# High and low halves of the weights interleaved column by column, with a shifted base and new homes for the early raw units

## What is computed

```python
mod = silu_c @ w_mod[l] + b_mod[l]
...
z_rec = h @ w_in[:, :REC_COLS]
z_rest = h @ w_in[:, REC_COLS:]
merged = jax.nn.sigmoid(ga) * (y_a @ w_pa) + jax.nn.sigmoid(gb) * (y_b @ w_pb)
return merged @ w_o, s_f, s_b
...
a, b = jnp.split(h @ w_up, 2, axis=-1)
return (jax.nn.silu(a) * b) @ w_down
...
proj = jnp.einsum('btd,de->bte', u, w_in[l])
y = jnp.einsum('bte,ed->btd', mixed, w_out[l])
```

## Time and profile before

| | us |
|---|---|
| median of 2 runs | 2324.36 |
| the runs | 2323.56 and 2325.15 |
| span of the profiled execution | 2323.0 |
| TensorE matmuls busy | 2264.8 |
| VectorE busy | 1633.6 |
| ScalarE busy | 995.5 |

### The profile page before, as it was taken

How to read it: one execution, slowest core, us unless ns; L and a number is a source line. 1 busy time by engine, 2 the same in 40 slices (tenths; PEclk the granted TensorE clock), 3 DMA queues, 4 the chain that set the end, 5 groups by cost and what they waited for, 6 DMA issues and landing times.

```text
span 2323.0 us, 48644 instructions
## 1 busy us (share of the span) xinstructions
PE 2264.8 (97%) x18378; PEld 2180.9 (94%) x18378; DVE 1633.6 (70%) x2515; ACT 995.5 (43%) x1402; POOL 8.4 (0%) x18
## 2 busy tenths in 40 slices
PE   5899999999999999989999999999999999999999
PEld 3678888999999999989999999999999999999999
DVE  4465564899976666988888887865557666667764
ACT  3322222555543434454444444444445444444452
POOL 0000000000000000000000000000000000000000
PEclk8999999999999999999999999999999999999999
DMA  9965455444356667975454555555556444444443
GB/s 406 389 252 218 181 223 210 164 145 144 144 217 236 258 236 287 344 306 197 181 181 181 185 187 188 185 198 180 184 192 217 156 153 147 160 146 161 146 179 128
DMA packets 69511, 475.62 MB, mean 205 GB/s; under 512 B 7728, under 2 KB 9776, under 8 KB 18384
## 3 DMA queue, kind: packets, MB, share of 16 engines
q1 hardware_dynamic: 68688, 467.59, 54.9%
q0 software_dynamic: 768, 7.26, 0.9%
HBM read 469.58 MB, written 5.24 MB: 204 GB/s over the span
## 4 chain that ended last, share of the span: by engine, by line
PE 88%; DVE 4%; ACT 1%; issue 1%; DVEq 0%; ACTq 0%
PE acc L795 83%; PE aux L795 4%; DVE lo L1157 1%; DVE ar L1384 0%; DVE qla L1377 0%; PE aux L1052 0%; ACT hi L462 0%; DVE raw L1167 0%; DVE qlb L1377 0%; DVE qs L1426 0%; DVE hxu L1174 0%; ACT n L666 0%; DVE n L1498 0%; ACT tt L594 0%; PE aux L887 0%
## 5 line engine op out<-in xcount | busy, mean ns | idle before, releaser
L1157 DVE TENSOR_TENSOR lo<-raw,hi 128x1024 fp32r<-128x1024 f32 (+1 forms) x716 | 811.9, 1167 | 196.8 <-ACT hi L462 192.2
L462 ACT ACTIVATE hi<-raw 128x1024 fp32r<-128x1024 f32 (+1 forms) x716 | 695.7, 1012 | 313.9 <-PE acc L795 259.9
L795 PE MATMUL acc<-hx,hi 128*128 128x256 f32 (+1 forms) x3072 | 662.7, 312 | 7.5 <-DVE lo L1157 4.1
L795 PEld LDWEIGHTS acc<-hx,hi 128*128 128x128 f32 x3072 | 496.1, 189 | 44.4 <-issue 6.9
L795 PE MATMUL acc<-hxu,hi 128*128 128x256 f32 x2816 | 502.7, 282 | 7.6 <-DVE hxu L1174 7.5
L795 PE MATMUL acc<-hx,lo 128*128 128x256 f32 (+1 forms) x1536 | 474.2, 309 | 0.0
L795 PEld LDWEIGHTS acc<-hxu,hi 128*128 128x128 f32 x2816 | 432.5, 189 | 8.8 <-issue 7.4
L795 PE MATMUL acc<-hxu,lo 128*128 128x256 f32 x1408 | 394.5, 280 | 0.0
L795 PE MATMUL acc<-u,hi 128*128 128x272 f32 (+1 forms) x2048 | 382.3, 287 | 0.0
L795 PEld LDWEIGHTS acc<-u,hi 128*128 128x128 f32 x2048 | 317.4, 188 | 4.5 <-issue 2.5
L795 PEld LDWEIGHTS acc<-hx,lo 128*128 128x128 f32 x1536 | 289.5, 189 | 17.5
(11 more groups left out here) (291 smaller groups left out, 2285.0 us busy)
## 6 DMA issues: line engine op xcount, KB each, us to landing
raw<-wts SPq DMA_DIRECT2D x390, 1024.0 KB, 4.8
raw<-wdown SPq DMA_DIRECT2D x64, 704.0 KB, 4.1
xc<-xct SPq DMA_DIRECT2D x1, 4096.0 KB, 12.3
rawx<-wts SPq DMA_DIRECT2D x2, 1024.0 KB, 24.7
x<-xct SPq DMA_DIRECT2D x1, 2048.0 KB, 9.8
park<-x POOLq DMA_DIRECT2D x1, 2048.0 KB, 10.4
xf<-park POOLq DMA_DIRECT2D x1, 2048.0 KB, 9.6
outt<-outs SPq DMA_DIRECT2D x16, 128.0 KB, 3.3
```

Of the source, the lines that this page charges most:

```text
L462: A.activation(HI[:, slot, a:b, 0:P], RAW[:, p % 4, a:b, :], ACT.Copy).then_inc(hi_half, 1)
L795: return pe.matmul(*a, **k)
L1157: V.tensor_tensor(LO[:, slot, a:b, 0:P], RAW[:, p % 4, a:b, :], HI[:, slot, a:b, 0:P].bitcast(F32), ALU.subtract).then_inc(lo_half, 1)
```

## The change

HI and LO become one tile HL in which column c of the high half and column c of the low half are neighbours: a row for one k has 2 x 128 + 16 = 272 words (1088 bytes). `half` is the view that ScalarE and VectorE write and read, `weights` the 128 columns, two words apart, that a matmul loads. HL starts at 32 KiB + 64 bytes and ends where HX begins. RAWX becomes two places of 8 KiB at 193 and 168, away from the weights. The second lies over SQ1, so SP waits for `sq1_read` to reach 4 before it loads it; the wait between the two early `lo` halves goes.

```diff
-PW = P + 8
+PAIR = 2 * P + 16
+HLROW = 2 * 16 * PAIR - 16
...
-        HI = at("hi", 32, [P, 2, 16, PW], F32R)
-        LO = at("lo", 49, [P, 2, 16, PW], F32R)
+        HL = at("hl", 32 + 1 / 16, [P, HLROW], F32R)
...
-        RAWX = at("rawx", 49.5, [P, 2, 17, P])
+        RAWX = [at("rawx0", 193, [P, 16, P]), at("rawx1", 168, [P, 16, P])]
...
+        def half(slot, a, b, part):
+
+            first = (slot * 16 + a) * PAIR + part
+            return bass.AP(HL[:].tensor, first, [[HLROW, P], [PAIR, b - a], [2, P]])
+
+        def weights(slot, k, part):
+
+            first = (slot * 16 + k) * PAIR + part
+            return bass.AP(HL[:].tensor, first, [[HLROW, P], [2, P]])
...
             for s in range(2):
-                sp.dma_start(RAWX[:, s, 0:16, :], wts[UNIT0["rec"] + 2 * s]).then_inc(raw_early[s], 16)
+                if s:
+                    sp.wait_ge(sq1_read, 4)
+                sp.dma_start(RAWX[s][:], wts[UNIT0["rec"] + 2 * s]).then_inc(raw_early[s], 16)
...
-                    A.activation(HI[:, slot, a:b, 0:P], RAW[:, p % 4, a:b, :], ACT.Copy).then_inc(hi_half, 1)
+                    A.activation(half(slot, a, b, 0), RAW[:, p % 4, a:b, :], ACT.Copy).then_inc(hi_half, 1)
...
-                        mm(o, HI[:, slot, k, 0:P], xh(k), start=first, stop=False)
-                        mm(o, HI[:, slot, k, 0:P], xl(k), start=False, stop=False)
-                        ins = mm(o, LO[:, slot, k, 0:P], xh(k), start=False, stop=last)
+                        mm(o, weights(slot, k, 0), xh(k), start=first, stop=False)
+                        mm(o, weights(slot, k, 0), xl(k), start=False, stop=False)
+                        ins = mm(o, weights(slot, k, 1), xh(k), start=False, stop=last)
...
-                    V.tensor_tensor(LO[:, slot, a:b, 0:P], RAW[:, p % 4, a:b, :], HI[:, slot, a:b, 0:P].bitcast(F32),
+                    V.tensor_tensor(half(slot, a, b, 1), RAW[:, p % 4, a:b, :], half(slot, a, b, 0).bitcast(F32),
                                     ALU.subtract).then_inc(lo_half, 1)
...
                         dve.wait_ge(hi_half, 2 * (i - 1) + h + 1)
-                        if h:
-                            dve.wait_ge(lo_half, 2 * i - 1)
-                        V.tensor_tensor(LO[:, i - 1, a:b, 0:P], RAWX[:, i - 1, a:b, :], HI[:, i - 1, a:b, 0:P].bitcast(F32),
+                        V.tensor_tensor(half(i - 1, a, b, 1), RAWX[i - 1][:, a:b, :], half(i - 1, a, b, 0).bitcast(F32),
                                         ALU.subtract).then_inc(lo_half, 1)
```

More of the change, by code:

```diff
@@ L517, in _ @@
                     for a, b in ((0, 8), (8, 16)):
-                        A.activation(HI[:, i - 1, a:b, 0:P], RAWX[:, i - 1, a:b, :], ACT.Copy).then_inc(hi_half, 1)
+                        A.activation(half(i - 1, a, b, 0), RAWX[i - 1][:, a:b, :], ACT.Copy).then_inc(hi_half, 1)
             act.sem_inc(raw_full[0], 16)
@@ L851, in early @@
                     o = ACC[:, s, :].rearrange("p (s t) -> p s t", s=2)
-                    mm(o, HI[:, s, k, 0:P], xch(k), start=k == 0, stop=False)
-                    mm(o, HI[:, s, k, 0:P], xcl(k), start=False, stop=False)
-                    ins = mm(o, LO[:, s, k, 0:P], xch(k), start=False, stop=k == KD - 1)
+                    mm(o, weights(s, k, 0), xch(k), start=k == 0, stop=False)
+                    mm(o, weights(s, k, 0), xcl(k), start=False, stop=False)
+                    ins = mm(o, weights(s, k, 1), xch(k), start=False, stop=k == KD - 1)
                     if k == KD - 1:
```

## The result

| | before | after |
|---|---|---|
| median, us | 2324.36 | 2347.93 |
| runs, us | 2323.56 and 2325.15 | 2343.57 and 2352.29 |
| span of the profiled execution, us | 2323.0 | 2350.5 |

The kernel became slower: ratio 1.0098, 95% interval 1.0065 to 1.013. The prediction was 2263 us. Its range, 2165 to 2350, holds the time; its sign was wrong. The profiled execution after is the slower of the two, by 8.7 us.

What follows compares the result with a forecast made beforehand. Bound: TensorE's 16,320 weight matmuls times their step. 2323.0 - 65 (load's surcharge) + 3 (waits for `lo`) + 0.5 (early units) = 2261.5 us profiled, 2263 us as median; range 2165 to 2350.

Steps and rivals of the forecast that it cites:

- What bounds the kernel: TensorE: the time is the number of weight matmuls, 16,320, times the step from one to the next.
- The surcharge: Each 256-column weight matmul carries 9 to 12 ns the array doesn't need, 147 us in all at 9 ns.
- a = 4.3 ns: The weight load's part of the surcharge per matmul, taken as the gain: 65 us after 7% deducted.
- rival 1: No effect: the moving stream may hinder itself, b = 7.4 ns per 256 columns; 2325 us, chance 0.22.
- The two streams run in step: Weight load and moving operand keep a fixed distance, 0 for only 1200 of 16,320 matmuls; gain 65 us.
- Strided reads are free: From VectorE's rows, 1.04 ns an element strided or contiguous; used as evidence against a slower strided weight load.
- rival 3: Slower: the strided load beside every matmul sets the step once over 118 ns; 2415 to 3750 us, chance 0.18.
- price ladder: Cost if the strided load sets the step: 90 us at 125 ns, 1430 us at 213 ns.
- Strided writes: ScalarE's copies and VectorE's subtractions: taken as 0 extra, bounds 0 and 8%, covered by idle time.
- The 3 us allowed: Allowance for TensorE waiting for `lo` if the cover of strided writes fails; bounds 0 and 20 us.
- The early units: At the start, SP's wait delays the second early load: 0.5 us, bounds 0 and 1.1.
- Marks to look for: Profile signs: 768 matmuls near 87.8 us if right; unchanged, near 84 or above 91 us if wrong.

Runs made afterwards that it cites:

- e9: Kernel before, but every weight load of the products reads one column 128 times; 2297.7 us.
- e13: Kernel before, with one column as moving operand of all three matmuls; steps 111.7 ns (256 columns) and 215.9 ns (512).
- e3: Kernel after without SP's wait (second early unit at 125.5 KiB), weights' base at 32 KiB; 2334.55 us.
- e4: Kernel after without SP's wait, weights' base at 32 KiB + 32 bytes; its time isn't stated in the text.
- e17: Like e16, but weights' base at 32 KiB exactly; 2309.28 us, 0.5% under the kernel before.
- e16: Kernel after without SP's wait, high and low halves of a k in two contiguous blocks, right weights; 2317.45 us.
- e8: Kernel after without SP's wait, base 32 KiB, no row padding of weights and activations except attn's U2; 256-column step 120.0 ns outside attn.
- e12: Kernel before (contiguous halves) without padding of the weights' and activations' rows; 2342.22 us.
- e15: Kernel after without SP's wait, loads contiguous but stores still strided, so weights are mixed and wrong; 2318.56 us.
- e2: Kernel after with the second early unit at 125.5 KiB and SP's wait gone; 2343.11 us, ratio 1.008.
- e14: Kernel after without SP's wait, one column as moving operand of all three matmuls; steps 117.6 ns (256 and 272 columns), 215.9 ns (512).
- e10: Like e8, but loads step 16 bytes instead of 8, giving wrong weights; 4057.19 us.
- e1: Kernel before (contiguous weights) with only the early units' new homes and SP's wait; 2327.48 us, ratio 1.0011.
- e11: Like e3, but attn's U2 64 bytes lower; attn got the kernel after's steps, its time isn't stated.
- e7: Kernel after, unchanged, run once more; 2345.99 us, ratio 1.0081.

## Why the prediction was wrong, and where it was right

**What bounds the kernel: right.** The time is the number of weight matmuls times their step; every kernel here followed the mean step of its phases, apart from the start.

**The surcharge: real, attributed wrongly.** The term a = 4.3 ns "for each load" came from two equations in two unknowns, which assume that both widths pay the same way. Measured, the load's running over memory is worth 2.2 ns (e9), and in `up` a one-column moving operand brings the step from 118.3 to 111.7 (e13), for 512 columns from 232.4 to 215.9. Most of the surcharge goes with the moving stream's running over memory; rival 1 had named that part. Had 2.2 ns gone on all 15,120 matmuls, the gain would have been 33 us and not 65.

**"The two streams run in step": the first step that failed.** It was taken to mean that they stop meeting, and that the load's share, the 4.3 ns, goes. A shorter repeating pattern did come. But the share didn't go (119.5 to 119.7 ns in `up` after, 118.3 before), and which relation one gets decides the size: from 118.3 to 120.6 ns in `up` with strided loads (e3, e4), 116.1 or 118.3 with dense ones (e17, e16), 120.0 without padding either way (e8, e12). The padding before spreads the pattern over 8 k and takes a mean of 118.3. And the same addresses gave two values (116.9 and 118.3 in `merge`, e15 and e16). A chosen relation was no better than that mean until a row showed it.

**"Strided reads are free", rival 3: the second step that failed, and the one that turned the sign.** The sum put the load's stride at nothing, on another engine's row. It costs 25 to 26 us (e2 against e16, e3 against e17); against the kernel before the loss was 17.8, since the new base and rows with dense loads gain 7.5 (e16). Rival 3 had the place and the threshold: the load beside every matmul, deciding once 128 columns take longer than the 118 ns step. Alone it takes 117.6 ns (e14): just under. That already caps the gain on 256 columns, by an estimate from these two steps, at 0.7 ns of 118.3, 13,632 x 0.7 = 9.5 us, whatever the streams do. With the moving stream on top the step became 119.5, 1.2 ns or about 1% more. The evidence against it was VectorE's reads, which didn't carry over to TensorE's. Of the price ladder in the prediction (125 ns: +90 us; 213 ns: +1430 us) the 16-byte step took 233 ns (e10) and +1730 us.

The estimate from the Trainium skill ("TensorE: Matmul & The Clock Gate", section "LDWEIGHTS (loading the stationary operand)"), 107 ns for 128 columns, and the prediction's remark that a load 11% slower would show, turned out near the truth: 117.6 / 107 = 1.10, though no run here shows 107 itself; the contiguous load took at most 111.7. The note of the Trainium skill's "SBUF — State Buffer" (DMA port swizzle, on cachelines), by which a step of 8 bytes keeps its speed, does not hold for this load: it lost at least 5.9 ns. Nor does its rule that TensorE's ports wait on nobody (section "Who interferes with whom") cover these rows: the step depended on the distance between load and moving stream by 2 ns.

**Strided writes: right in effect, half right in size.** VectorE paid nothing (1219 to 1220 ns for 1024 elements). ScalarE paid 10% (1054 to 1159 ns for the same), beyond the 8% bound, which came from another engine's row. Of the mark "VectorE's and ScalarE's mean times stay" only VectorE's part held. All was hidden, as said: dense writes (e16) against strided ones (e15) are 2317.45 against 2318.56 us. The 3 us allowed for it were not needed.

**The early units: mis-sized.** The forecast was 0.5 us, bounds 0 and 1.1; e1 measured 2.2 (0.2 to 4.9 by its interval, 2325.32 x 0.0001 to 0.0021), so it may lie within the bounds too. The bound asked only when the early unit's data would flow. It left out what is behind the wait on SP: the next mod1 unit went out 8.8 us later and landed 1.6 us late, the later ones about 2 (e1) or up to 7 and more (the profile after).

**Marks to look for.** "Runs above 91 us for 768 (rival 3)" is what came: 91.95. "Attn's 48 of 256 stay or rise": 5.66 to 5.69. "The second early unit lands near 30": 31.4.

**Left open:** why a matmul steps in 112.5 in one place and 120.0 in another, and what picks one of two patterns at the same addresses. No rule was found that gives the step from the two addresses, and e11's repair of attn (120.5 to 118.3) is one case, not a rule.

## What to carry to other kernels

Where TensorE's step is near the time of a weight load, keep the 128 weights of a load contiguous: a stride of two words is enough to make the load the bound at 256 columns (117.6 ns), four words double the time. Use a row of the engine in question as evidence for a stride; VectorE's row misled for TensorE and for ScalarE. The relative address of weights and moving data was worth up to 2% of a float32r step here and can't be reasoned out from these rows, but it costs one constant to try. Take several executions when you do, and compare steps of more than one profile: the same addresses gave 116.9 and 118.3 ns. A wait put into the queue that feeds a DMA-bound stage is priced by everything queued behind it.

## What the runs showed of the hardware that wasn't expected

- A float32r matmul pays at least 6.6 ns (256 columns, where the load may be the bound without it) or 16.5 ns (512) for a moving operand that runs over memory rather than staying on one column (e13 against before).
- 128 weights 16 bytes apart load in about 233 ns, 8 bytes apart in 117.6, contiguous in 111.7 at most: the first doubling of the step costs at least 5%, the second another 98%.
- With rows of exactly 1024 or 512 bytes a k the mean 256-column step in up, down and proj was 120.0 ns, with interleaved (e8) and contiguous weights (e12) alike; the 512-column step moved in opposite directions, 233.3 and 227.0 against 232.4.
- At the same addresses a long stretch runs in one of several repeating patterns of steps: `merge` in 119.7 or 119.5 ns (after and e7, the same kernel), in 116.9 or 118.3 (e15 and e16, whose stores and weights' values differ).
- The first 24 matmuls after a stall (they start at 129 to 138 us) ran in 3.11 us in e3 and 5.46 us in e2, at a granted clock of 1.00 and 0.89 over the stretch from 120 to 150 us. That isn't the addresses: the kernel after took 5.46 us in its profile and 4.49 in e7's.
